# Modulation sums of the first feed-forward network: buffers and a queue of their own, ScalarE multiplies, GpSimd adds

## The reference, cut to what matters

```python
c_act = jax.nn.silu(c)                      # (1, 1024)
mod = c_act @ mod_w[layer] + mod_b[layer]   # mod_w[layer]: 1024 x 6144, two layers
sh1, sc1, g1, sh2, sc2, g2 = jnp.split(mod, 6, axis=-1)
u = modulate(rms_norm(h, norm_ffn[layer]), sh2, sc2)
h = h + g2[:, None, :] * swiglu(u, ffn_w_in[layer], ffn_w_out[layer])
# after layer 0: shift, scale = split(c_act @ kv_mod_w + kv_mod_b); k, v from modulate(rms_norm(h)) @ w_kv
def swiglu(u, w_in, w_out):                 # w_in: 1024 x 5632, w_out: 2816 x 1024
    gate, up = jnp.split(u @ w_in, 2, axis=-1)
    return (jax.nn.silu(gate) * up) @ w_out
```

## Time and profile before

| what | value |
|---|---|
| median of 3 runs | 2322.44 us (2321.78 to 2323.91) |
| the profiled execution, its own time | 2321.61 us |
| its span in the trace | 2319.6 us |
| TensorE busy / VectorE / ScalarE / GpSimd | 2189.9 / 1410.4 / 752.1 / 424.3 us |
| TensorE's mean granted clock | 0.975 of full speed |

### The profile page before, as it was taken

How to read it: one execution, slowest core, us unless ns; L and a number is a source line. 1 busy time by engine, 2 the same in 40 slices (tenths; PEclk the granted TensorE clock), 3 DMA queues, 4 the chain that set the end, 5 groups by cost and what they waited for, 6 DMA issues and landing times.

```text
span 2319.6 us, 25720 instructions
## 1 busy us (share of the span) xinstructions
PE 2189.9 (94%) x10094; PEld 1752.1 (76%) x10094; DVE 1410.4 (61%) x1929; ACT 752.1 (32%) x961; POOL 424.3 (18%) x272
## 2 busy tenths in 40 slices
PE   7899999979999997999989999998999998999997
PEld 5588788767888886866678888876568876888885
DVE  5666766554767767177455444467565776655656
ACT  1443334332222223256432222244233333322321
POOL 0000000039998873200000000000420000000000
PEclk9999999989999998999999999999999998999998
DMA  6343231225555542422122322322112221323220
GB/s 245 124 161 109 92 127 57 71 84 188 200 182 182 182 163 94 143 91 74 52 76 91 99 101 91 109 94 69 41 48 98 92 81 65 109 91 109 91 91 37
DMA packets 39327, 249.54 MB, mean 108 GB/s; under 512 B 4627, under 2 KB 4819, under 8 KB 11112
## 3 DMA queue, kind: packets, MB, share of 16 engines
q1 hardware_dynamic: 32856, 230.97, 28.7%
q0 software_dynamic: 3008, 10.63, 1.4%
q10 hardware_dynamic: 3344, 6.29, 0.7%
HBM read 241.58 MB, written 6.29 MB: 107 GB/s over the span
## 4 chain that ended last, share of the span: by engine, by line
PE 81%; DVE 8%; issue 4%; POOL 3%; ACT 2%; DMA 1%; SPq 0%; ACTq 0%; DVEq 0%; POOLq 0%
PE bank L680 24%; PE bank L682 23%; PE bank L681 23%; PE bank L907 2%; DVE w_lo L1847 2%; PE bank L727 1%; ACT w_hi L1373 1%; PE bank L1025 1%; PE bank L1035 1%; PE bank L1046 1%; POOL raw L593 1%; PE bank L714 1%; DMA raw<-in_wts 1%; PE bank L823 1%; POOL raw L594 1%
## 5 line engine op out<-in xcount | busy, mean ns | idle before, releaser
L680 PE MATMUL bank<-u_hi,w_hi 128*128 128x512 f32 x1708 | 695.1, 407 | 40.3 <-DVE w_lo L1847 11.8
L682 PE MATMUL bank<-u_hi,w_lo 128*128 128x512 f32 x1708 | 672.9, 394 | 0.0
L681 PE MATMUL bank<-u_lo,w_hi 128*128 128x512 f32 x1708 | 672.8, 394 | 0.0
L1847 DVE TENSOR_TENSOR w_lo<-raw,w_hi 128x2048 fp32r<-128x2048 f32 x162 | 427.8, 2641 | 225.9 <-ACT w_hi L1373 225.8
L680 PEld LDWEIGHTS bank<-u_hi,w_hi 128*128 128x128 f32 x1708 | 325.8, 191 | 129.6 <-issue 49.0
L1373 ACT ACTIVATE w_hi<-raw 128x2048 fp32r<-128x2048 f32 x162 | 309.1, 1908 | 341.6 <-PE bank L682 300.4
L682 PEld LDWEIGHTS bank<-u_hi,w_lo 128*128 128x128 f32 x1708 | 325.0, 190 | 70.0
L681 PEld LDWEIGHTS bank<-u_lo,w_hi 128*128 128x128 f32 x1708 | 326.1, 191 | 67.0 <-issue 3.8
L680 PE MATMUL bank<-g_hi,w_hi 128*128 128x512 f32 x772 | 306.2, 397 | 13.8 <-DVE w_lo L1847 6.4
L681 PE MATMUL bank<-g_lo,w_hi 128*128 128x512 f32 x772 | 301.8, 391 | 0.0
L682 PE MATMUL bank<-g_hi,w_lo 128*128 128x512 f32 x772 | 301.7, 391 | 0.0
(11 more groups left out here) (284 smaller groups left out, 2262.0 us busy)
## 6 DMA issues: line engine op xcount, KB each, us to landing
raw<-in_wts SPq DMA_DIRECT2D x218, 1024.0 KB, 4.8
spectra<-pool ACTq DMA_DIRECT2D x16, 256.0 KB, 2.0
scr<-in_rel POOLq DMA_DIRECT2D x16, 256.0 KB, 3.4
pool<-spectra POOLq DMA_DIRECT2D x16, 256.0 KB, 3.0
H<-in_x ACTq DMA_DIRECT2D x1, 2048.0 KB, 21.3
out<-H SPq DMA_DIRECT2D x8, 256.0 KB, 2.0
pool<-in_window POOLq DMA_DIRECT2D x1, 1024.0 KB, 9.1
pool<-in_filt_w POOLq DMA_DIRECT2D x1, 512.0 KB, 6.2
```

The costliest lines, as they stand in the source:

```text
L680: pe.matmul(out, lh, rh, start=start, stop=False, skip_group_check=True)
L681: pe.matmul(out, lh, rl, start=False, stop=False, skip_group_check=True)
L682: return pe.matmul(out, ll, rh, start=False, stop=stop, skip_group_check=True)
L1847: dve.tensor_tensor(w_lo[RING[w]][:, :], raw[W_STREAM[w] % raw_ring][:, :], w_hi[RING[w]][:, :].bitcast(F32), ALU.subtract).then_inc(lo_do ...
```

## The change

The pooled M slots leave the stream of the `raw` buffers: `RING_ITEMS` holds the weight slots and the first 20 M slots alone. The other 36 get three buffers of their own, `m_buf`, cut out of a working area that is free in this stage, and are loaded by GpSimd's own DMA queue (`load_mod`): three as soon as the first product of the `wo0` projection (the stage ahead of the norm before FFN0) is there, then slot m + 3 when slot m has been summed. The multiply moves from GpSimd to ScalarE: right after the split of the weight slot that `M_BEFORE` names, `scale_mod` does eight ACTIVATE instructions of 128x256 in place, each with a column of `cact` as scale and a zero column as bias. GpSimd keeps the three additions, and waits for the eight of ScalarE (`m_scaled`).

```diff
--- before.py
+++ after.py
@@ -152,8 +152,14 @@
         W_LIST.append(_s[1:])
     else:
         M_BEFORE.append(len(W_LIST))
-W_STREAM = [s for s, item in enumerate(STREAM) if item[0] == "W"]
-M_STREAM = [s for s, item in enumerate(STREAM) if item[0] == "M"]
+RING_ITEMS = []
+_m = 0
+for _s in STREAM:
+    _m += _s[0] == "M"
+    if _s[0] == "W" or _m <= M_POOLED:
+        RING_ITEMS.append(_s)
+W_STREAM = [s for s, item in enumerate(RING_ITEMS) if item[0] == "W"]
+M_STREAM = [s for s, item in enumerate(RING_ITEMS) if item[0] == "M"]
 NW = len(W_LIST)
 NM = len(M_BEFORE)
 NVMOD = NM // 4
@@ -382,6 +388,7 @@
         ar = Arena()
         ff_s = view(ar(2 * SEQ), 2, SEQ)
         ff_h = view(ar(2 * SEQ), 2, SEQ)
+        m_buf = [pool[:, a:a + SLOT] for a in (4096, 6144, 12288)]
         Facc = view(ar(KC * SEQ), KC, SEQ)
 
         ar = Arena()
@@ -445,6 +452,8 @@
             sem(x) for x in ("vec_in", "filt_in", "x_in", "mask_in", "rel_in0", "rel_in1", "m_in"))
         rel_in = [rel_in0, rel_in1]
         rel_ready, mask_ready, taps_in = sem("rel_ready"), sem("mask_ready"), sem("taps_in")
+        m_scaled = sem("m_scaled")
+        mod_in = [sem(f"mod_in{x}") for x in range(3)]
         const_ready = sem("const_ready")
         cact_ready, lb_d, lb_e, lb_ready = sem("cact_ready"), sem("lb_d"), sem("lb_e"), sem("lb_ready")
         h_upd, sq_done, sq_add = sem("h_upd"), sem("sq_done"), sem("sq_add")
@@ -548,7 +557,7 @@
             sp.dma_start(f_w2[0:FH, :, :], A["filt_w23"]).then_inc(filt_in, 16)
             where = []
             w = m = 0
-            for s, item in enumerate(STREAM):
+            for s, item in enumerate(RING_ITEMS):
                 if s >= raw_ring:
                     kind, n = where[s - raw_ring]
                     if kind == "W":
@@ -582,20 +591,29 @@
                 links[0] += 1
                 pl.wait_ge(plink, links[0])
 
+            def load_mod(m):
+
+                i = m - M_POOLED
+                pl.dma_start(m_buf[i % 3], A["wts"][M_SOURCE + m]).then_inc(mod_in[i % 3], 16)
+
             def sum_mods():
 
+                pl.wait_ge(product, READY[FIRST["wo0"]])
+                for m in range(M_POOLED, M_POOLED + 3):
+                    load_mod(m)
                 pl.wait_ge(u_l, U_FFN0 + KC)
                 for m in range(M_POOLED, NM):
-                    s = M_STREAM[m]
-                    src = raw[s % raw_ring]
-                    pl.wait_ge(raw_in[s % raw_ring], 16 * (s // raw_ring + 1))
-                    chunks = src[:, :].rearrange("p (k c) -> p k c", k=KC)
-                    link(pl.tensor_tensor(chunks, chunks, cact[:, :].unsqueeze(2).broadcast_to((P, KC, 256)), ALU.mult))
+                    i = m - M_POOLED
+                    src = m_buf[i % 3]
+                    pl.wait_ge(m_scaled, KC * (i + 1))
                     link(pl.tensor_tensor(src[:, 0:1024], src[:, 0:1024], src[:, 1024:2048], ALU.add))
                     link(pl.tensor_tensor(src[:, 0:512], src[:, 0:512], src[:, 512:1024], ALU.add))
                     if m >= MRING:
                         pl.wait_ge(mod_sum, m - MRING + 1)
                     pl.tensor_tensor(macc[:, m % MRING, :], src[:, 0:256], src[:, 256:512], ALU.add).then_inc(m_pooled, 1)
+                    if m + 3 < NM:
+                        pl.wait_ge(m_pooled, i + 1)
+                        load_mod(m + 3)
 
             pl.memset(zcol[:, 0:1], 0.0).then_inc(const_ready, 1)
             pl.memset(zcol[:, 1:2], EPS).then_inc(const_ready, 1)
@@ -1360,6 +1378,14 @@
 
         @block.scalar
         def _(act):
+            def scale_mod(m):
+
+                i = m - M_POOLED
+                act.wait_ge(mod_in[i % 3], 16 * (i // 3 + 1))
+                for k in range(KC):
+                    x = m_buf[i % 3][:, k * 256:(k + 1) * 256]
+                    act.activation(x, x, ACT.Identity, bias=zcol[:, 0:1], scale=cact[:, k:k + 1]).then_inc(m_scaled, 1)
+
             fed = [0]
 
             def feed(upto):
@@ -1371,6 +1397,9 @@
                     if PREV[w] is not None:
                         act.wait_ge(product, USED[PREV[w]])
                     act.activation(w_hi[RING[w]][:, :], raw[s % raw_ring][:, :], ACT.Copy).then_inc(hi_done, 1)
+                    for m in range(M_POOLED, NM):
+                        if M_BEFORE[m] == w:
+                            scale_mod(m)
                     fed[0] += 1
 
             def ahead(label, i):
```

## The result

| | before | after |
|---|---|---|
| median, runs of one comparison | 2322.11 us (2321.43 to 2323.91) | 2297.54 us (2296.14 to 2298.91) |
| ratio, 95% interval | | 0.9887 [0.9873, 0.9901] |
| profiled execution / span | 2321.6 / 2319.6 us | 2296.9 / 2294.9 us |
| mean granted clock | 0.975 | 0.979 |

The change made the kernel 24.6 us (1.1%) faster. I had forecast 22.8 us and 2299.6 us. The mechanism came out as forecast in the main; the sum was a little short and the range's lower edge too near.

What follows compares the result with a forecast made beforehand. TensorE bounds the kernel, losing time in FFN0 to late `w_lo` and before the norm to slowed squares. A 9.5 + B 3.7 + C 0.9 + E 3.3 + D 5.2 + 0.2 = 22.8 us won, giving 2299.6 us, range 2297 to 2307.

Steps and rivals of the forecast that it cites:

- A: FFN0 at 524.47: TensorE's 6.8 us wait for `w_lo` of fi2, then half clock; 9.5 us to be won.
- B: FFN0 at 560.66: TensorE's 2.0 us wait for a bank, then a reduced clock; 3.7 us to be won.
- C: FFN0 at 506.12: TensorE's wait for `w_lo` of fi1; 0.9 us to be won.
- modelled ends: TensorE's three waits begin at modelled matmul ends, so are worth up to 0.5 us more; 0.2 counted.
- E: FFN0's 25 slots from 565.10 to 852.87: small losses in the fo slots, 3.3 us, all taken as won.
- D: End of FFN0: VectorE's additions of squares before the norm, slowed beside GpSimd's multiplies; 5.2 us to be won.
- The loads: M slot loads on GpSimd's queue: 9.1 us to landing, some 50 us of lead for the first three; hidden.
- FFN1's comparison: FFN0 against FFN1, for the same 33 slots: 17 to 18 us lost in FFN0; the terms found sum to 17.4.
- rival 1: ScalarE's multiplies cost near 6.5 us per M slot, so `w_lo` of fi3 stalls TensorE: 2305 us; chance 0.10.
- rival 2: GpSimd's additions still fall on `w_lo` and squares; E stays, perhaps 2 of A to C return: 2303 to 2305; chance 0.13.
- rival 3: M slot loads land late (over 24 us) and ScalarE holds up the next split; at 28 us, 2344; chance 0.05.
- rival 4: Waits only shifted: another engine takes A's place, only D and part of E won: 2312 to 2318; chance 0.06.

Runs made afterwards that it cites:

- experiment 2: The changed kernel, but GpSimd multiplies as before, with the own buffers and queue kept: 2328.4 us, ratio to before 1.0019.
- experiment 5: The changed kernel with each ScalarE ACTIVATE on the first 32 of these M slots done twice: 2313.5 us, ratio to before 0.9956.
- experiment 8: The changed kernel, but ScalarE multiplies only the last four M slots (m = 52 to 55), GpSimd the others: 2309.0 us, ratio to before 0.9938.
- experiment 9: The changed kernel, but ScalarE multiplies only m = 20 to 23 and 52 to 55, GpSimd the 28 between: 2304.8 us, ratio to before 0.9926.
- experiment 6: The changed kernel plus one unneeded GpSimd multiply and addition beside the squares before the norm: 2306.4 us, ratio to before 0.9930; again, 2305.1 us.
- experiment 4: The changed kernel, ScalarE still multiplying, but M slots back in the shared `raw` buffers, loaded by SyncE: 2438.9 us in one run.
- experiment 7: The changed kernel, but TensorE's small matmuls for m = 46 to 51 moved to the gap before the norm: 2298.9 us, ratio to before 0.9895.
- experiment 3: The changed kernel, but M slots loaded from SyncE's queue into the same three own buffers: 2298.3 us, ratio to before 0.9893.

## Why the prediction was nearly right, and where it failed

- **A, B, C (14.1, and 0.2 of the modelled ends): right.** 14.5 us came back. The split of fi3 began at 518.35 where I had 522.4, 1.15 of it because FFN0 began earlier and 2.4 because eight ACTIVATEs take 4.0 us and not 4.8. So `w_lo` had more to spare than I had walked. The sums of m = 22 had less, 1.2 us in place of 1.9: I had let GpSimd's additions run alone, and one waited for VectorE. It is these sums that TensorE waited for in experiments 2, 5 and 8. fo0's sums were forecast for 550.6; they stand at 549.46, in an execution that began FFN0 1.15 us earlier, so at the very place. Of the 0.5 for modelled ends 0.4 came, where I had counted 0.2.
- **E: the term that was mis-sized**, 3.3 us where 3.9 were measured. I had taken 11.38 us, one fi slot of before, as the length of an undisturbed slot. Undisturbed it is 283.83 / 25 = 11.35, and the 0.03 count 25 times. Its cause was in part only argued. I had put E down to GpSimd's multiply beside `w_lo`, but in the profile of experiment 2 GpSimd multiplied and E was gone all the same. That a slow `w_lo` is lost time in the fo slots is true only at some of them (experiment 9).
- **D: right**, 5.2 forecast and 5.1 measured (the last two additions of squares take 1.48 together, undisturbed, where I had 2 x 0.68); experiment 6 takes 4.2 of it away again by one multiply and one addition.
- **The loads: right that they are hidden**, by far more than needed, and on whichever queue. The rule of the Trainium skill against this queue (SBUF — State Buffer, SBUF: two separate sides) shows no price here: 5.2 us to landing, 4.9 on SyncE's queue, and the same stretch on either. The section names VectorE operations in a two-port mode for it, and no row here tells in which mode VectorE ran, so the rule is neither confirmed nor refuted. That two engines take turns at the memory, from the same section, agrees with the rows of every run in which GpSimd multiplies.
- **The range: the step that failed.** I wrote that below the forecast there is "only what FFN1's comparison leaves, 1 us, and another 1.5 for the spread of executions". The terms were short by 0.8 us (E by 0.6, the modelled ends by 0.2), which the 1 us covered. By the ratio the time came out 3.4 us below the forecast, so 2.6 were left for spread where I had allowed 1.5; the early start of FFN0 makes 1.1 in the profiled execution. But the executions of this one kernel ran from 2296.1 to 2302.2 us, so 1.5 was too little: the first comparison came out at 2296.2 and the second at 0.9902 x 2322.44 = 2299.7. That the first fell below the edge and the second on the forecast is luck of the draw.
- **The rivals.** 1 fell with 4.03 us for eight. 2 fell too, in its price: GpSimd's additions cost TensorE nothing at 5 us a slot, though they do meet VectorE; the multiply costs at the ends (experiments 2 and 8) and 0 to 4 us between. 3 fell by the 5.2 us of its loads. 4 fell by the first view of waits: nothing took A's place.

What I had not seen is how much the parts depend on one another. I priced the multiply's move by ScalarE's spare time and by E and D. Experiments 2 and 4 show that either half of the change by itself wins nothing (2328 and 2439 us).

## What to carry to other kernels

When a buffer that throttled an engine is taken away, ask what that engine will do next and beside what: in experiment 2 GpSimd, freed of the shared buffers, ran its last multiplies straight into the chain that ended the stage. Price a moved operation at the tightest place (a double slot, the end of a stage) and not by the average slot; by the profiled stretch, 28 of the 36 M slots could have kept the slow version for 1.8 us, though the median of that kernel was 5 to 7 us over the change's. And where a change touches one stage, compare profiles by the distance between two fixed instructions around it: here that repeated to 0.05 us for the change, where whole executions differed by 6. Where the stretch itself holds waits, take more than one profile.

## What the runs showed of the hardware that was not expected

Between the first two profiles of the changed kernel, the spread behind the stretch is the clock. In a stage far behind the change, at 1671 us, TensorE waits 1.87 us for VectorE, in both. TensorE's timeline in the first profile, and then the window of 8 us from there:

```profile
1671.15 1.12 PE L1184 MATMUL bank<-pool 128*128 128x512 f32 x2 [1.87 <-DVE pool L2370]
...
1672.80 1.02 PE L1184 MATMUL bank<-pool 128*128 128x512 f32 x2
```

```profile
1671.00:1679.00 8.00, 7.85 (x38) 5.84 (x38) 6.81 (x13) 0.00 (x0) 2.58 (x3) 1.00 0.13 23
```

and in the second, from the same instruction on:

```profile
1673.49 1.13 PE L1184 MATMUL bank<-pool 128*128 128x512 f32 x2 [1.87 <-DVE pool L2370]
...
1675.30 1.91 PE L1184 MATMUL bank<-pool 128*128 128x512 f32 x2
```

```profile
1673.34:1681.34 8.00, 7.85 (x32) 5.64 (x33) 5.48 (x10) 0.00 (x0) 1.04 (x1) 0.79 0.00 0
```

The same wait was followed by full clock (2.4 GHz) in one execution and by a stretch at half clock (1.2 GHz) in the other: 38 matmul records against 32 in the 8 us, and the next norm's columns come 239.9 us after this matmul in the first and 243.0 in the second. From profile to profile of kernels that don't differ there I find such steps of 1.6, 2 and 3 us at three places, which make the 1414.7 to 1421.3 us of the table. They are not alike. The step of 3 us, the one shown here, parts the first two profiles of the change, and the two of the kernel of experiment 6. The steps of 1.6 and 2 stand in every profile of experiments 5 to 8, both of experiment 6 among them, and in none of the three of the change, of experiment 3 or of before. So they repeat with the kernel as far as the profiles go, and are not shown to be spread. What decides at any of the three no run here shows.

A second thing: how short an operation can be and still wait a whole turn. VectorE's 0.68 us became 4.21 beside a multiply that began 0.04 us after it by the records, and 4.11 beside one that began 0.04 us before it; so at such distances the records don't tell who gets the turn.
